# A feed-forward phase cut into four units of seven products and three half units, instead of two plain units, three of seven products and one half unit

## The reference

```python
def swiglu(x, w_gu, w_down):                     # w_gu: 1024 x 5632, w_down: 2816 x 1024
    gate, up = jnp.split(x @ w_gu, 2, axis=-1)
    return (jax.nn.silu(gate) * up) @ w_down

x = x + 0.5 * swiglu(rmsnorm(x, ffn1_norm[i]), ffn1_w_gu[i], ffn1_w_down[i])
x = x + mixer_i(rmsnorm(x, mix_norm[i]))
x = x + 0.5 * swiglu(rmsnorm(x, ffn2_norm[i]), ffn2_w_gu[i], ffn2_w_down[i])
```

## Time and profile before

| | |
|---|---|
| median of three runs | 2085.04 us |
| the profiled execution, its own time | 2082.98 us |
| its span, first to last instruction | 2080.2 us |
| TensorE busy | 2035.5 us (98%) |
| VectorE busy | 1549.4 us (74%) |
| ScalarE busy | 1176.8 us (57%) |
| GpSimd busy | 144.7 us (7%) |
| DMA | 419.87 MB, 202 GB/s |

### The profile page before, as it was taken

One profiled execution on the slowest core, in us unless ns is written; L12 is line 12 of the kernel. 1 busy time (PEld: TensorE's weight loads), 2 busy tenths in 40 slices (PEclk: granted clock), 3 DMA queues, 4 the chain that ended last, 5 costly groups with the idle time before them and its releaser, 6 DMA issues.

```text
span 2080.2 us, 25402 instructions
## 1 busy us (share of the span) xinstructions
PE 2035.5 (98%) x10385; PEld 1717.4 (83%) x10385; DVE 1549.4 (74%) x1488; ACT 1176.8 (57%) x1231; POOL 144.7 (7%) x160
## 2 busy tenths in 40 slices
PE   7999999999999999999999999999999999999998
PEld 6887987887888889988887888988878887988886
DVE  6778556877887778868878877778778877557776
ACT  6556555655665566646555555446555556556554
POOL 1000000000100012211001000000001000001000
PEclk9999999999999999999999999999999999999999
DMA  8867523877787384457876867658877876425863
GB/s 269 264 216 226 167 97 109 244 254 222 213 252 205 124 262 128 129 210 214 251 212 195 242 241 187 200 195 248 242 223 195 250 206 231 151 81 134 257 225 103
DMA packets 242183, 419.87 MB, mean 202 GB/s; under 512 B 10668, under 2 KB 92932, under 8 KB 241556
## 3 DMA queue, kind: packets, MB, share of 16 engines
q1 hardware_dynamic: 216020, 363.65, 51.6%
q0 software_dynamic: 26048, 54.61, 14.6%
HBM read 417.14 MB, written 1.08 MB: 201 GB/s over the span
## 4 chain that ended last, share of the span: by engine, by line
PE 83%; DVE 9%; ACT 4%; issue 3%; POOL 1%; DMA 0%; SPq 0%; POOLq 0%; DVEq 0%; ACTq 0%
PE bank L1492 51%; PE bank L1605 18%; PE bank L1498 7%; DVE w_lo L1052 4%; ACT w_hi L703 3%; PE bank L1639 2%; DVE arena L1363 2%; PE bank L1778 1%; DVE arena L1136 1%; PE bank L1770 1%; PE bank L1525 1%; POOL yms L613 0%; DMA stage<-in_ffn_w_gu 0%; ACT arena L949 0%; PE bank L1771 0%
## 5 line engine op out<-in xcount | busy, mean ns | idle before, releaser
L1052 DVE TENSOR_TENSOR w_lo<-stage,w_hi 128x2048 fp32r<-128x2048 f32 (+1 forms) x225 | 509.5, 2266 | 186.5 <-ACT w_hi L703 185.2
L1052 DVE TENSOR_TENSOR w_lo<-arena,w_hi 128x2048 fp32r<-128x2048 f32 (+1 forms) x196 | 444.2, 2267 | 174.1 <-ACT w_hi L703 173.3
L703 ACT ACTIVATE w_hi<-stage 128x2048 fp32r<-128x2048 f32 (+1 forms) x225 | 425.3, 1892 | 220.1 <-PE bank L1492 146.7
L703 ACT ACTIVATE w_hi<-arena 128x2048 fp32r<-128x2048 f32 (+1 forms) x196 | 371.9, 1898 | 242.6 <-PE bank L1492 160.0
L1492 PE MATMUL bank<-w_hi,mt_hi 128*128 128x512 f32 (+1 forms) x944 | 373.1, 395 | 1.3 <-DVE mt_lo L1253 1.1
L1492 PE MATMUL bank<-w_lo,mt_hi 128*128 128x512 f32 (+1 forms) x944 | 366.8, 389 | 0.0
L1492 PE MATMUL bank<-w_hi,mt_lo 128*128 128x512 f32 (+1 forms) x944 | 366.3, 389 | 0.0
L1492 PE MATMUL bank<-w_hi,xt_hi 128*128 128x512 f32 x704 | 280.2, 398 | 2.1 <-DVE w_lo L1052 2.1
L1492 PE MATMUL bank<-w_lo,xt_hi 128*128 128x512 f32 x704 | 276.0, 392 | 0.0
L1492 PE MATMUL bank<-w_hi,xt_lo 128*128 128x512 f32 x704 | 251.7, 390 | 0.0
L1492 PEld LDWEIGHTS bank<-w_hi,mt_lo 128*128 128x128 f32 x944 | 178.4, 189 | 37.3
(11 more groups left out here) (198 smaller groups left out, 2754.3 us busy)
## 6 DMA issues: line engine op xcount, KB each, us to landing
arena<-in_ffn_w_gu SPq DMA_DIRECT2D x81, 1024.0 KB, 5.3
stage<-in_ffn_w_gu SPq DMA_DIRECT2D x79, 1024.0 KB, 5.3
stage<-in_ffn_w_down SPq DMA_DIRECT2D x96, 512.0 KB, 4.7
arena<-in_ffn_w_down SPq DMA_DIRECT2D x80, 512.0 KB, 5.0
arena<-in_ffn_w_gu POOLq DMA_DIRECT2D x29, 1024.0 KB, 9.8
stage<-in_ffn_w_gu POOLq DMA_DIRECT2D x19, 1024.0 KB, 9.7
stage<-in_ffn_w_gu SPq DMA_DIRECT2D x18, 512.0 KB, 8.9
stage<-in_sb_w_qkv SPq DMA_DIRECT2D x16, 512.0 KB, 4.3
```

Source lines behind the costliest of these rows:

```text
L703: act.activation(w_hi[q][:, 0:c], stage[s][:, 0:c], ACT.Copy).then_inc(hi_done, 1)
L1052: dve.tensor_tensor(w_lo[q][:, 0:c], stage[s][:, 0:c], w_hi[q][:, 0:c].bitcast(F32), ALU.subtract).then_inc(lo_done, 1)
```

## The change

`UNITS` goes from `PSHSPS` to `HSHSHSS` and `DOWNS` follows. The phase has 45 blocks in place of 42. Where two summed units follow one another the waits between units are those of S. In the vector program, the low part of the phase's last block (`split(b0 + i + 2)` at A4 of the last unit) is made ahead of the low parts of the last unit's hidden columns (`hidden_lo`) instead of behind them.

```diff
--- before.py
+++ after.py
@@ -48,8 +48,8 @@
 SSD_STAGE_SLOTS = 3
 
 
-UNITS = "PSHSPS"
-DOWNS = (0, 2, 1, 2, 2, 1)
+UNITS = "HSHSHSS"
+DOWNS = (0, 1, 2, 1, 2, 1, 1)
 
 
 def unit_col(u):
@@ -1199,6 +1199,8 @@
                         part_sum(u, hid[:, 1, :], bank[6][:, :], p16, 3, ALU.add)
                         hidden_summed(u, 0)
                         hidden_summed(u, 1)
+                        if u == N_UNITS - 1:
+                            split(b0 + i + 2)
                     for v in range(N_UNITS):
                         if TURNED_AFTER[v] == i:
                             hidden_lo(v)
@@ -1210,7 +1212,7 @@
                         released(*FFN_ORDER[i - 1], i - 1)
                     if i == 1 and N_SUMS:
                         x_sums()
-                    if i + 2 <= len(FFN_ORDER):
+                    if i + 2 <= len(FFN_ORDER) and (i == 0 or FFN_ORDER[i - 1] != (N_UNITS - 1, "A2")):
                         split(b0 + i + 2)
                     if i + 2 < len(FFN_ORDER):
                         u, name = FFN_ORDER[i + 2]
@@ -1556,6 +1558,8 @@
 
                     if u == 0:
                         return
+                    if u == 1 and UNITS[0] == "H":
+                        up_banks_free(0)
                     if UNITS[u - 1] == "P":
                         pe.wait_ge(silu_done, 2 * (N_UNITS * f + u))
                     elif UNITS[u - 1] == "H":
@@ -1632,6 +1636,8 @@
 
                 def hidden_transpose(u):
                     pe.wait_ge(gated, 2 * (N_UNITS * f + u + 1))
+                    if u == 0:
+                        up_banks_free(0)
                     for b in range(down_parts(u)):
                         for c in range(2):
                             for h in range(HALVES):
@@ -1643,9 +1649,9 @@
                 for i, (u, name) in enumerate(FFN_ORDER):
                     n = b0 + i
                     block_in(n)
-                    if name in ("G0", "G1") and u == 0:
+                    if name in ("G0", "G1", "H0", "H1") and u == 0:
                         first_block(n, int(name[1]))
-                        if name == "G1" and p == 0:
+                        if name[1] == "1" and p == 0:
                             pe.wait_ge(xg_done, QUARTERS)
                             mixer_vectors_to_channels()
                     elif name in ("G0", "G1", "H0", "H1"):
```

## The result

| | before | after |
|---|---|---|
| median of four runs | 2084.98 us | 2259.41 us |
| lowest to highest | 2083.68 to 2085.62 | 2257.61 to 2263.36 |
| ratio, 95% interval | | 1.084 (1.0826 to 1.0855) |
| span of the profiled execution | 2080.2 us | 2255.6 us |
| TensorE, VectorE, ScalarE busy | 98%, 74%, 57% | 92%, 74%, 55% |

The changed kernel is slower by 174 us, 8.4%, and 2259 us had been forecast. The forecast hit the number, yet one of its terms was wrong by 14 us and another by about as much the other way.

The account below looks back on a forecast made before the run. TensorE, 98% busy, was taken as the bound; waits of 24.7 us per phase less 2.7 of matmuls gave 22.0, over eight phases (some 2 us less in the first) 174 us more, so 2259 us, range 2208 to 2310.

Parts of the forecast that it names:

- start: 7.8 + 1.7 + 1.6: Phase start: 7.8 us waiting at B11 and A1, 1.7 at D0 behind unit 0's turning, 1.6 for half clock.
- H beside S, two turnings: Units 3 and 5: D of the unit just turned waits for VectorE's hidden low part, 2.6 us, twice 5.2.
- one D where two were: Units 1, 3 and 5: one D block between A1 and A4's weight sum delays A2 and A4, 2.9 us a phase.
- S to H, twice: Half unit behind a summed one: H0 waits for the join that frees bank 5, 0.67 us, twice 1.3.
- S to S: Unit 5 to 6: weight sum ahead of the joins delays B11 2.85 us, A1 0.9, B22 and D0 0.4: 4.2.
- moved low part: Phase end: the moved low part fills VectorE's idle 1.38 us and delays the last hidden low parts 0.7; net nothing.
- 12 matmuls less: Each feed-forward phase has 744 matmuls in place of 756, all on TensorE's path: 2.7 us saved.
- The DMA: A2's accumulating load lands about when VectorE is free for the sum that reads it; costed at nothing.
- the clock: Granted clock falls to half at each phase's start, after the 5.9 us pause; cost 1.6 us a phase.
- The third rival: Short pauses at two turnings and unit 6 also halve the clock, about 2 us each: 48 more, 2307; chance 0.14.
- The first rival: Waits stay hidden in VectorE's 37 idle us a phase; 22 us gained, 2063 us; chance 0.04.
- The second: Rival: only the phase's start costs, D blocks and joins slip through; 8.4 us a phase, 2150 us; chance 0.10.

Follow-up runs that it names:

- experiment 3: Changed kernel with 24 idle matmuls into an unused bank in the pause ahead of each phase's first B11: 2253.45 us, ratio 1.0814.
- experiment 5: Changed kernel with VectorE making the half unit's products ahead of A1's low part at the phase's start: 2242.24 us, ratio 1.0766.
- experiment 4: Changed kernel with the D blocks spread otherwise, none right behind its own unit's turning: 2155.65 us, ratio 1.0341.
- experiment 6: Kernel before with two DOWNS entries exchanged, so its half unit's D stands directly behind that unit's turning: 2119.8 us, ratio 1.0174.
- Experiment 2: Kernel before with the moved low part alone: 2069.25 us, ratio 0.993.
- experiment 1: Changed kernel with the moved low part put back in front of the joins of A4: 2268.32 us, ratio 1.0884.

## Why the prediction was right, and where it was not

The sum held, phase by phase: 22.3 us on the mean of the seven phases where 22.0 was forecast, 19.2 in the first where 20 was. By steps, mean of those seven phases, with what half clock added in them and in a column of its own:

| step of the prediction | forecast, us | measured, us | of it half clock |
|---|---|---|---|
| start: 7.8 + 1.7 + 1.6 | 11.1 | 11.4 | 2.0 |
| H beside S, two turnings | 5.2 | 6.5 | 1.4 |
| one D where two were | 2.9 | 2.8 | |
| S to H, twice | 1.3 | 1.5 | |
| S to S | 4.2 | 4.7 | 0.4 |
| moved low part | 0 | -1.8 | |
| 12 matmuls less | -2.7 | -2.7 | |
| sum | 22.0 | 22.4 | 3.8 |

The measured values are the blocks' spacings less their matmuls and transposes, against those of the kernel before; the phases themselves give 22.3. The last column compares a stretch followed by a fall with the same stretch without one: for the turnings and S to S in the changed kernel itself, for the start in experiment 3.

*Start.* Right, also in size: 9.4 without the half clock where 9.5 was forecast. The order of VectorE that the prediction wrote out is the one in the trace; 5.66 was measured for 5.9. Experiment 3 shows the parts without half clock, and experiment 5 that the order of two of its pieces is worth 17 us.

*Turnings.* Right in mechanism: three a phase, 2.35 us of idle TensorE at the second of the fourth phase, 2.6 by the spacing of the blocks. Experiments 4 and 6 show it from both sides.

*A2 and A4, S to H.* Right within 0.1 us each.

*S to S.* Right where the clock holds (2.9 at B11, 0.9 at A1, 0.3 behind); with half clock A1 starts 4.4 to 5.4 late in place of 3.8, and all but once that eats what comes behind, so that only 0.1 to 0.4 us are lost.

*The DMA.* Costed at nothing, and nothing waits for it.

**The step that failed** is the one on the moved low part, "Cost and gain nothing". The low part that moves had been misread. I took it for one that had only filled idle time; it is the one that stood between the joins of the last unit. With it out of the way the last join and the gated products come 2.2 us earlier and TensorE's last transposes 1.8, and the 1.59 us of the earlier trace rows are gone. That wait stood in my own rows: I cited it as what the rest of the phase consists of and used it against a rival, and didn't ask what stood ahead of it on VectorE, where the answer was one join waiting behind a low part. The step should have read -1.8 us a phase, -14 in all. Experiment 2 gives 15.3.

**The step that was too small** is the clock. It had one fall a phase; the trace has 26 ahead of the execution's end, in place of the 9 that this makes with the one of the SSD phase. The third rival, given 0.14, was true in part: of the 16 turnings of units 2 and 4, six (pauses of 2.6 us) were followed by a fall, and so were six of the eight pauses of 2.9 at unit 6. At a turning a fall cost 1.6 us, near the rival's 2. From the D block behind one turning to that behind the next it is the same work, and it takes 51.99 us without a fall and 53.63 with one:

```profile
589.75 0.47 PE L1494 MATMUL bank<-w_hi,mt_hi 128*128 128x512 f32 x1 [2.15 <-DVE mt_lo L1142]
...
641.74 0.47 PE L1494 MATMUL bank<-w_hi,mt_hi 128*128 128x512 f32 x1 [2.35 <-DVE mt_lo L1142]
...
695.37 0.47 PE L1494 MATMUL bank<-w_hi,mt_hi 128*128 128x512 f32 x1 [2.36 <-DVE mt_lo L1142]
```

At unit 6 it cost 0.1 to 0.4 us in five phases and 1.6 in the fourth. So the rival's "each" was wrong in both. Added up over the eight phases, such comparisons give an estimate of 16 us at the starts (with five falls behind the turning of unit 0), 10 at the other turnings and 3 at unit 6: some 29 us for the 13 forecast. With the small rests of the other steps that is 2.2 us a phase more (26.9 us of waits for 24.7), near the failed step's size with the other sign. With only one of the two steps right it would have been off by some 15 us; that the total agrees within 1 us is luck.

Two readings of the prediction don't hold. It called the one fall inside the work of the kernel before agreement with a rule on waits between bursts; but TensorE was busy for all of the 3.4 us ahead of that fall, with narrow matmuls and no wait. And the lower end of its range, 2208, doesn't follow from the terms that it names: 13 and 13 below 2259 is 2233.

The first rival (faster) fell as expected: 2.7 us against 27. The second (only the start costs, 2150) fell with the 24 waits for L1142.

The 29 us are an estimate from one execution; the 112 us more at half clock than before allow no more than 56. No experiment took the half clock out everywhere and left the waits: experiment 4 took both, and in experiment 3 falls came at other pauses. Idle matmuls at the turnings of units 2 and 4, where the program has bank 7 free, were not tried.

## What to carry to other kernels

Where one engine prepares what another consumes, a sum of idle time says nothing: 37 us free a phase didn't hide 15 us of work, because here each piece could start only when its consumer had finished something else. Write the preparing engine's order out from the place where it is released and see when each result is due; that gave every new group of waits here, in number and within 0.3 us in size where the clock held; it missed the one wait that went away. And ask of each wait in the rows what stands ahead of its releaser on that engine: one instruction of 2.2 us taken from between the joins, with no other change, made the kernel before faster by 15 us (2069.25 against 2084.55), and was the only part of this change that was seen to do so.

## What the runs showed of the hardware

**The clock fell after pauses of 2.6 us, but not each time.** The timeline and the windows view of the fourth phase in the changed kernel, at a turning and where units 5 and 6 meet:

```profile
641.74 0.47 PE L1494 MATMUL bank<-w_hi,mt_hi 128*128 128x512 f32 x1 [2.35 <-DVE mt_lo L1142]
...
718.36 0.77 PE L1609 MATMUL bank<-w_hi,xt_hi 128*128 128x512 f32 x1 [2.68 <-DVE arena L1136]
```
```profile
641.50:647.50 6.00, 5.76 (x18) 4.63 (x19) 2.39 (x2) 0.37 (x1) 0.00 (x0) 0.72 1.09 330
718.40:723.00 4.60, 4.60 (x11) 3.64 (x12) 3.82 (x5) 4.18 (x4) 1.61 (x2) 0.50 0.66 97
```

At the first the matmul starts at full clock, 0.47 us long, and the granted clock falls while TensorE is already at work (0.72 over the six microseconds); at the second it is 0.50 (1.2 GHz) from the first matmul on. After 1.59 us of idle in the kernel before it never fell, in eight phases. The same pause in the same program was followed by a fall in one phase and not in the next; what decides it stays open. The mean granted clock also differs between runs of one kernel, and the time with it: by 16 us in the four runs of experiment 1 (0.969 to 0.978), by 2 to 8 in the other runs on the changed kernel, against 10 in eleven runs of the kernel before on that chip. The Trainium skill (TensorE: Matmul & The Clock Gate, section "A second HAM failure mode") tells of short idle times between groups of matmuls that make the clock swing. The trace before had nothing of it; the trace after agrees, with 12 such places in 24.
